# One kernel, two blocks of layers: pooling and a convolution's norm run inside the head norms, and a bias table is built inside the attention that reads it

## What is computed

```python
def _pool_branch(u, grid, pool_w, pool_scale):
    ...
    for g, win in enumerate(POOL_WINDOWS):
        ch = uf[..., g * POOL_GROUP:(g + 1) * POOL_GROUP]
        groups.append(_centred_mean(ch, axis, win) - ch)
    pooled = jnp.stack(groups, axis=-2)
    mixed = jnp.einsum('...gi,gio->...go', pooled, pool_w)
    return mixed.reshape(b, n, D_POOL) * pool_scale

def conformer_conv(a_val, a_gate, conv_w, conv_b, ln_g, ln_b):
    u = a_val * jax.nn.sigmoid(a_gate)
    u = dwconv(u, conv_w, conv_b)
    return jax.nn.silu(layer_norm(u, ln_g, ln_b))

    q = axial_rope(rms_norm(q, qn_g))
    k = axial_rope(rms_norm(k, kn_g))

def neighborhood_attn(q, k, v, kc, vc, rpb):
    ...
    bias = rpb[:, dr_idx[:, None, :, None], dc_idx[None, :, None, :]]
    s_win = jnp.einsum('brqhd,brkwhd->bhrqkw', qg, kb).astype(jnp.float32) * scale \
        + bias.astype(jnp.float32)[None]
```

## Time and profile before

| what | us |
|---|---|
| median of three executions | 6007.8 (6003.9 to 6013.1) |
| the profiled execution | 6002.6 |
| its span in the trace | 6000.8 |
| PE busy (share of the span) | 5150.4 (86%) |
| DVE busy | 3387.5 (56%) |
| ACT busy | 1902.3 (32%) |
| POOL busy | 1751.2 (29%) |

### The profile page before, as it was taken

One profiled execution on the slowest core, in us unless ns is written; L12 is line 12 of the kernel. 1 busy time (PEld: TensorE's weight loads), 2 busy tenths in 40 slices (PEclk: granted clock), 3 DMA queues, 4 the chain that ended last, 5 costly groups with the idle time before them and its releaser, 6 DMA issues. The chain is left out here.

```text
span 6000.8 us, 127551 instructions
## 1 busy us (share of the span) xinstructions
PE 5150.4 (86%) x55385; PEld 3990.6 (67%) x55385; DVE 3387.5 (56%) x5084; ACT 1902.3 (32%) x3017; POOL 1751.2 (29%) x1377
## 2 busy tenths in 40 slices
PE   6799999699998466587999857999988999979989
PEld 1488888488888355466888634555557788766667
DVE  2236656444444566467699246888864300057877
ACT  1224444133332443133211223444430300026652
POOL 1201111254443655024200004666642511100012
PEclk8899999799999788888999978999999999989999
DMA  6334434411211110365332231000045321131035
GB/s 204 104 110 151 148 140 149 139 60 52 64 54 59 64 57 26 119 198 153 104 107 94 78 129 45 22 17 17 13 152 167 102 77 68 70 105 63 31 113 161
DMA packets 430189, 568.20 MB, mean 95 GB/s; under 512 B 66870, under 2 KB 318646, under 8 KB 417166
## 3 DMA queue, kind: packets, MB, share of 16 engines
q1 hardware_dynamic: 365158, 387.20, 20.6%
q10 hardware_dynamic: 49272, 115.65, 5.0%
q0 software_dynamic: 15216, 57.44, 2.4%
HBM read 357.07 MB, written 203.12 MB: 93 GB/s over the span
## 5 line engine op out<-in xcount | busy, mean ns | idle before, releaser
L157 PE MATMUL p_bank<-p_hT_high,p_w_high 128*128 128x512 f32 (+1 forms) x2784 | 1053.0, 378 | 19.7 <-DVE p_w_low L151 15.8
L159 PE MATMUL p_bank<-p_hT_high,p_w_low 128*128 128x512 f32 (+1 forms) x2784 | 1044.8, 375 | 0.0
L158 PE MATMUL p_bank<-p_hT_low,p_w_high 128*128 128x512 f32 (+1 forms) x2784 | 1044.7, 375 | 0.0
L157 PEld LDWEIGHTS p_bank<-p_hT_high,p_w_high 128*128 128x128 f32 x2784 | 525.2, 189 | 123.1 <-DVE p_w_low L151 16.2
L159 PEld LDWEIGHTS p_bank<-p_hT_high,p_w_low 128*128 128x128 f32 x2784 | 525.1, 189 | 94.8
L158 PEld LDWEIGHTS p_bank<-p_hT_low,p_w_high 128*128 128x128 f32 x2784 | 525.5, 189 | 93.2
L2832 POOL TENSOR_TENSOR at_acc<-at_acc,at_p 128x512 f32<-128x512 f32 x256 | 423.9, 1656 | 144.1 <-ACT at_p L2770 122.6
L2770 ACT ACTIVATE at_p<-at_sc 128x1024 f32<-128x1024 f32 (+1 forms) x296 | 284.9, 1013 | 401.6 <-PE at_sc L2661 349.7
L1555 PE MATMUL rsc_db<-rsc_W,rsc_TK 64*64 64x64 f32 x8640 | 383.7, 219 | 6.2 <-issue 6.0
L2874 DVE TENSOR_REDUCE at_mx<-at_mb 128x2 f32<-128x1024 f32 (+1 forms) x280 | 342.3, 1222 | 81.3 <-PE at_mb L2672 79.2
L157 PE MATMUL o_bank<-o_w_high,o_m_high 128*128 128x512 f32 x800 | 314.4, 393 | 63.7 <-POOL o_m_low L151 63.7
(11 more groups left out here) (419 smaller groups left out, 10627.9 us busy)
## 6 DMA issues: line engine op xcount, KB each, us to landing
rsc_X<-rwkv_chunks SPq DMA_DIRECT2D x108, 320.0 KB, 4.7
pT<-p_o ACTq DMA_DIRECT2D x132, 256.0 KB
rwkv_chunks<-p_arr POOLq DMA_DIRECT2D x54, 512.0 KB, 5.4
o_z<-pT SPq DMA_DIRECT2D x50, 512.0 KB, 5.3
o_y<-y SPq DMA_DIRECT2D x50, 512.0 KB, 6.5
pT<-p_eo ACTq DMA_DIRECT2D x96, 256.0 KB
p_w<-in_w_in_dram SPq DMA_DIRECT2D x33, 512.0 KB, 4.3
x<-o_o ACTq DMA_DIRECT2D x32, 512.0 KB
```

Source lines behind the costliest of these rows:

```text
L157: nc.tensor.matmul(out, lhs[0], rhs[0], start=start, stop=False)
L158: nc.tensor.matmul(out, lhs[0], rhs[1], start=False, stop=False)
L159: return nc.tensor.matmul(out, lhs[1], rhs[0], start=False, stop=stop)
```

## The change

Three stages lose their own block.

- **pool** goes. Its work is a class `Pooling`, which `head_norm` calls ahead of its own work on each engine in the stage hn: first the pooling's loads, then item 0's, and so on. The second tile `u[1]` is loaded after the constants, with a semaphore of its own, and the results are written over the tiles `u`. PE uses the banks of the odd items; the wait for them (`released`) stands ahead of item 1.
- **cf** goes. Its work is a class `Conformer`, called the same way at the head of stage qk. Gates 2 to 4 move into the loop over the items, on ACT ahead of the squares of items 1 to 3 (`GATES_AT`). SP loads items 0 to 2, then issues the five stores of the chunks, each waiting for its gate, and only then loads anything else.
- The four pieces of the modulation move from pool to qk: SP issues their 8 loads behind the chunks' stores and ahead of the load of item 3; PE does piece 0 to 3 at the end of its turns 6 to 9, DVE adds the bias at the end of its turns 7 to 10, SP stores them last.
- **nat** goes. `one_hot` is loaded in four parts into tiles that the attention uses later, the raw biases come over ACT's queue, q, k and v are loaded right behind; PE and DVE build `bt` as before, in the banks of the scores; the scores of step 0 follow at once, and `bi` is made after the maxima of step 0 (steps 0 and 1 read `bt` only).

```diff
-def pool_branch(nc, PT, w, scale, inv_count, yT, later):
...
+class Pooling:
...
+    def loads(self, sp):
+        sp.wait_ge(self.zeroed, 3)
+        for t in range(2):
+            sp.dma_start(self.u[t][:, :, POOL_PAD:POOL_PAD + self.W],
+                         self.PT[t * P:(t + 1) * P, 0:SEQ].rearrange("p (r w) -> p r w", w=self.W)).then_inc(self.u_in[t], 16)
+            if t == 0:
+                sp.dma_start(self.cnt[:], self.inv_count).then_inc(self.const_in, 16)
+                sp.dma_start(self.sc[:], self.scale.rearrange("(t p) -> p t", p=P), allow_slow_non_contiguous=True).then_inc(self.const_in, 16)
                 for g in range(4):
                     h = g % 2 * HD
...
+                    sp.dma_start(self.wd[h:h + HD, g // 2, h:h + HD], self.w[g]).then_inc(self.const_in, 16)
+
+    def out(self, t):
+        return self.u[t][:].rearrange("p r w -> p (r w)")[:, 0:SEQ]
+
+    def stores(self, sp):
+        for t in range(2):
+            sp.wait_ge(self.scaled, 4 * (t + 1))
+            sp.dma_start(self.yT[t * P:(t + 1) * P, 0:SEQ], self.out(t)).then_inc(self.stored, 16)
...
+        for t in range(2):
+            dve.wait_ge(self.u_in[t], 16)
+            dve.wait_ge(self.const_in, 16 * 6)
...
-def head_norm(nc, name, items, mean_ones, gather, spread, rope=None):
+def head_norm(nc, name, items, mean_ones, gather, spread, rope=None, before=None, later=None):
...
+        first = before[0](nc, ctx, *before[1], banks[4:8])
+        MC = 384
+        PIECES = [c * MC for c in range(4, 3 * D // MC)] if later else []
...
+            mp = [*bank[1][1:4], bank[0][3]]
...
+                first.loads(sp)
                 load(0)
...
-                for n in range(2, NI):
+                load(2)
+                if later:
+                    sp.dma_start(cond[:, 0, :], mod_c[0].rearrange("(p k) -> p k", k=KT)).then_inc(cond_in, 16)
+                    sp.dma_start(cond[:, 1, :], mod_c_ctx.rearrange("(p k) -> p k", k=KT)).then_inc(cond_in, 16)
+                first.stores(sp)
+                for q, c in enumerate(PIECES):
+                    sp.dma_start(ms[q][:], mod_b[c:c + MC].partition_broadcast(2)).then_inc(mw_full[q], 16)
+                    sp.dma_start(mw[q][:], mod_w.rearrange("(p k) n -> p k n", k=KT)[:, :, c:c + MC]).then_inc(mw_full[q], 16)
+                for n in range(3, NI):
                     load(n)
+                for q, c in enumerate(PIECES):
+                    sp.wait_ge(mod_bias, q + 1)
+                    sp.dma_start(mod_out[:, c:c + MC], ms[q][:]).then_inc(mod_stored, 16)
+                first.finished(sp)
+                if later:
+                    sp.wait_ge(mod_stored, 16 * len(PIECES))
...
+                first.vector(dve)
                 dve.wait_ge(const_in, 16 * NCONST)
...
+                    q = n - (NI - 3)
+                    if 0 <= q < len(PIECES):
+                        dve.wait_ge(mod_sum, q + 1)
+                        dve.wait_ge(mw_full[q], 32)
+                        nc.vector.tensor_tensor(ms[q][:], mp[q][0:2, 0:MC], ms[q][:], ALU.add).then_inc(mod_bias, 1)
...
+                    if n == 1:
+                        first.released(pe)
...
+                first.tensor(pe)
                 pe.wait_ge(const_in, 16 * NCONST)
...
+                    q = n - (NI - 4)
+                    if 0 <= q < len(PIECES):
+                        pe.wait_ge(act_ready, 1)
+                        pe.wait_ge(mw_full[q], 32)
+                        for k in range(KT):
+                            mm = nc.tensor.matmul(mp[q][0:2, 0:MC], cond_act[:, k, :], mw[q][:, k, :], start=(k == 0), stop=(k == KT - 1))
+                        mm.then_inc(mod_sum, 1)
...
+                first.scalar(act)
+                if later:
+                    act.wait_ge(cond_in, 32)
+                    nc.scalar.activation(cond_act[:].rearrange("p k r -> p r k"), cond[:], ACT.Silu).then_inc(act_ready, 1)
...
+                    first.beside(act, n)
                     act.wait_ge(a_in[u], 16 * loads(n))
...
-def conformer(nc, ln_g, ln_b, mean_ones, yT):
+class Conformer:
...
+    GATES_AT = {1: 2, 2: 3, 3: 4}
...
+    def stores(self, sp):
+        for c, (t0, n) in enumerate(self.CHUNKS):
+            sp.wait_ge(self.acted, c + 1)
+            sp.dma_start(self.rows[:, :, t0:t0 + n], self.y[c][:, :, 0:n]).then_inc(self.stored, 16)
...
+    def beside(self, act, n):
+        if n in self.GATES_AT:
+            self.gate(act, self.GATES_AT[n])
...
+            if c == 2:
+                self.gate(act, 0)
+                self.gate(act, 1)
+
+    def gate(self, act, c):
+        n = self.CHUNKS[c][1]
+        act.wait_ge(self.normed, c + 1)
+        for t in range(self.NTL):
+            x = self.nc.scalar.activation(self.y[c][:, t, 0:n], self.y[c][:, t, 0:n], ACT.Silu, bias=self.pr[:, 1, t:t + 1], scale=self.pr[:, 0, t:t + 1])
+        x.then_inc(self.acted, 1)
...
-        with ExitStack() as ctx1:
-            s1 = Scope(nc, ctx1, "nat")
-            oh = s1.sb("oh", [64, ROW, P])
-            rp = s1.sb("rp", [64, NH, NDD])
-            raw = s1.sb("raw", [P, 64])
-            *ps, turned = s1.banks(5)
-            const_in, filled, rp_ready, prod, taken = (s1.sem(n) for n in ("const_in", "filled", "rp_ready", "prod", "taken"))
-            raw_in, raw_turned = s1.sem("raw_in"), s1.sem("raw_turned")
-            inner_ready, masked = s1.sem("inner_ready"), s1.sem("masked")
-            with nc.Block() as block:
-                @block.sync
-                def _(sp):
-                    sp.dma_start(idn[:], ident).then_inc(raw_in, 16)
-                    sp.wait_ge(filled, 1)
...
+        hot = [pt[u][0:64].rearrange("p a b c -> p (a b) c") for u in range(2)]
+        hot += [y[u][0:64].rearrange("p (n c) -> p n c", c=P) for u in range(2)]
+        table = [win[:, n // 2, n % 2, :] for n in range(4)]
...
+                sp.dma_start(idn[:], ident).then_inc(idn_in, 16)
+                for u in range(4):
+                    sp.dma_start(hot[u], one_hot[:, 16 * u:16 * u + 16, :]).then_inc(const_in, 16)
                 load_pair(0)
                 load_values(0)
...
+                pe.wait_ge(const_in, 16 * 4)
+                for n in range(ROW // 4):
+                    if n >= 4:
+                        pe.wait_ge(taken, n - 3)
+                    for i in range(4):
+                        x = nc.tensor.matmul(table[n % 4][:, i * P:(i + 1) * P], hot[n // 4][:, n % 4 * 4 + i, :], rp[:].rearrange("p h d -> p (h d)"),
+                                             start=True, stop=True)
+                    x.then_inc(prod, 1)
                 pe.wait_ge(zeroed, 1)
+                pe.wait_ge(taken, ROW // 4)
                 scores(0)
...
                 add(0)
                 maxima(0)
+                nc.vector.tensor_copy(bi[:], bt[:, :, 3:3 + R + 1, :]).then_inc(inner_ready, 1)
+                dve.wait_ge(inner_ready, 1)
+                nc.vector.memset(bi[0:64, :, R, :], MASK / SC).then_inc(masked, 1)
+                nc.vector.memset(bi[64:128, :, 0, :], MASK / SC).then_inc(masked, 1)
+                dve.wait_ge(masked, 2)
                 add(1)
...
+                act.wait_ge(filled, 1)
+                for half in range(2):
+                    act.dma_start(raw[0:NH * 15, 32 * half:32 * half + NDC], rpb.rearrange("h r c -> (h r) c")).then_inc(raw_in, 16)
                 keep_ctx(0)
...
-    pool_branch(nc, pT1, a["pool_w"][0], a["pool_scale"][0], a["inv_count"], y1, later[1])
...
-    head_norm(nc, "hn", items, a["head_mean"], a["head_gather"], a["head_spread"])
+    head_norm(nc, "hn", items, a["head_mean"], a["head_gather"], a["head_spread"], None,
+              (Pooling, (pT1, a["pool_w"][0], a["pool_scale"][0], a["inv_count"], y1)))
...
-    conformer(nc, a["ab_ln_g_2"][0], a["ab_ln_b_2"][0], a["mean_512"], y2)
...
-    head_norm(nc, "qk", items, a["head_mean"], a["head_gather"], a["head_spread"], (a["rope_cos"], a["rope_sin"], a["rope_swap"]))
+    head_norm(nc, "qk", items, a["head_mean"], a["head_gather"], a["head_spread"], (a["rope_cos"], a["rope_sin"], a["rope_swap"]),
+              (Conformer, (a["ab_ln_g_2"][0], a["ab_ln_b_2"][0], a["mean_512"], y2)), later[1])
```

More of the change, by code:

```diff
@@ L1283, with __init__ @@
 POOL_CH, POOL_PAD = 256, 8
-def pool_branch(nc, PT, w, scale, inv_count, yT, later):
+class Pooling:
     ROWS, W = SEQ // HD, HD
-    WP = W + 2 * POOL_PAD
-    with ExitStack() as ctx:
+    def __init__(self, nc, ctx, PT, w, scale, inv_count, yT, banks):
         s = Scope(nc, ctx, "pool")
[L1292 to L1310, removed]
-        with nc.Block() as block:
-            @block.sync
-            def _(sp):
[L1315 to L1320, removed]
@@ new lines, in tensor, with released @@
+    def tensor(self, pe):
+        for t in range(2):
+            pe.wait_ge(self.pooled_ready, t + 1)
+            for c in range(4):
+                if t:
+                    pe.wait_ge(self.scaled, c + 1)
```

(34 more changed lines are left out.)

334 lines of the change are left out of this document (126 added, 208 removed).

## The result

Four runs of the kernel after took 5942.7 to 5952.0 us, median **5946.2**; four of before, beside them, 5998.4 to 6013.1, median 6005.8. The forecast was 5957.7 (5936 to 5979) and faster.

What follows compares the result with a forecast made beforehand. TensorE was busy for 86% of the span, but barriers give each stage its own limit, with pool and cf chains of waits. Terms -66.9 + 29.4 - 28.2 + 21 + 7 - 12.4 = -50.1 gave 5957.7 us, range 5936 to 5979.

Steps and rivals of the forecast that it cites:

- Pool goes: Between p1 and rsc: rsc reads nothing that pool makes, so it starts where pool did, -66.9 us.
- Pooling at the head of hn: Start of hn: folding waits for DVE's window sums and starts 45.8 in, not 16.4, +29.4 us.
- Join of cf and qk: Head of qk: rotation constants are loaded early, so folding follows DVE's work on the chunks at once, -28.2 us.
- The gates: Gates 2 to 4 on ACT, between qk's roots and squares: hidden in ACT's idle time, nothing; uncovered, three would cost 16.
- Item 3 is late: In qk, item 3's load stands behind 6.3 MB of weights, so PE's sums of item 3 start later, +21 us.
- The pieces: End of qk, PE's turns 6 to 9: four modulation pieces of 5.24 each, partly hidden, +7 us.
- nat goes: Start of attention: first scores no longer wait for copies to `bi`, barrier and landing of q and k, -12.4 us.
- A: Rival in qk: item 3 is not late, sum -71.1, kernel 5937 us; chance 0.10.
- B: Rival in qk: pieces run at 1.2 GHz, 5.2 more each, about +20, kernel 5978 us; chance 0.13.
- C: Rival in qk: weights come at 154 GB/s, disturbed by POOL's stores, +24, kernel 5982 us; chance 0.07.
- D: Rival in qk: kernel slower, SP's queue holding item 3 back for 83 us; chance 0.03.
- E: Rival: untouched stages give the time back or joined stages start as late as before, 5996 to 6020 us; chance 0.04.

Runs made afterwards that it cites:

- e8: e7 with only the pads of `u` and the small matrix zeroed, counts loaded first, window sums not waiting for the matrix: ratio to before 0.9836, hn 149.85 us.
- e1: The kernel after with item 3's load issued ahead of the four weight loads in qk: ratio to before 0.9892, cf and qk 197.3 us.
- e2: The kernel after with the weight loads issued behind item 2's load, ahead of the chunks' stores: ratio to before 0.9867, cf and qk 187.2 us.
- e3: e2 with one matmul in place of eight in each modulation piece: executed once, cf and qk 181.3 us.
- e7: The kernel after with weights right behind the chunks' loads, item 3 ahead of the last chunk's store, pieces moved earlier: ratio to before 0.9831, cf and qk 176.9 us.

## Why the prediction was right

**Pool goes:** -66.9 to the tenth. The next stage, which reads nothing of it, starts as far behind p1 as pool did (7.6).

**Pooling at the head of hn:** +28.0 for +29.4. The mechanism is the one given (window sums, then folding, in one chain on DVE); the folding moved by 28.2. The sums started 14.8 after the first instruction, not 15.9, because the matrix landed 1 sooner. e8 shows that the chain sets the folding: 6.5 taken from its front bring the folding 6.4 forward. The rest of hn isn't the constant that it was taken for: it varies by some 3 either way, so the agreement of the whole stage to 1.4 is partly luck.

**Join of cf and qk:** the folding moved by 30.3 for 28.2. The other 2 lie in the chunks' own chain: DVE ends it 61.2 after the stage's start, where before it took 63.2. Why that chain got shorter wasn't looked into. The gates cost 0.6, not nothing. The argument (PE asks for square n only after item n - 2 is rotated) has no hold on square 1, since there is no item ahead of item 0, and gate 2 stands ahead of that square: PE waited 0.63 for it, which was one of the recorded signs of being wrong, if a small one. For gate 3 the argument held, with ACT still waiting 8.12 for PE before its root of item 2. The table load of 1.28 ahead of gate 4 is followed by its silu 1.30 after its start (3460.11, 3461.41), again with nothing behind it. The Trainium skill (ScalarE: Activation LUTs, What ACT_TABLE_LOAD costs) has 2.66 with a drain; the trace doesn't agree, here as in the earlier trace rows, and the measurement decides.

**Item 3 is late:** the sums of item 3 came 67.0 behind the folding in after and 46.5 before: +20.5, for +21. The mechanism and the size are right: PE's wait before them grew by 22.1, from 3.65 to 25.80, and square 3 began 26.7 behind the end of gate 4, where the sum had 26.0. (The "idle ACT of some 20" doesn't fit the prediction's own sum.) Against the 22.1, items 0 to 2 went 1.7 faster than before, which the sum didn't have: over item 0's sums PE's granted clock was 0.66 (5.54 us), before 0.57 (6.37). e1 and e2 show the cause and not only the coincidence: with the weights ahead of the need the wait falls by 20.7, with item 3 alone ahead most of it moves to item 4. The Trainium skill (DMA: Bandwidth & Descriptors, Two DMAs through the same engine are not ordered) says that within one queue of one DMA engine descriptors start in order; the trace agrees as far as it shows it, in that item 3, issued behind the weights, landed 14 after its issue at 373 GB/s, and in e1, issued ahead of them, 6 after it.

**The pieces:** +8.25 for +7, read from item 6's sums to the attention's first load (33.5 against 25.2); e3 shows the cause. Pieces 1 to 3 took 5.32, piece 0 took 7.48: until 3543.0 its granted clock was 0.50, as over item 6's sums ahead of it, and over piece 1 it was 1.00. The predicted end of piece 0 was 7.8 behind the start of those sums, and it was 8.6. (The 3.4 put down for eight records of 512 columns at full clock is 3.5 by the pieces' own 0.33 for 384, and 3.60 in after's trace; nothing hangs on it.)

**nat goes:** -13.4 for -12.4; the `one_hot` parts landed about 1 earlier than the whole did.

**What the sum missed.** Between the sums of item 3 and of item 6 after took 46.3 where before took 49.0 (-2.7). Most of it is one group of matmuls, the sums of item 4, in after and then before:

```profile
3508.48 3.72 PE L2311 MATMUL qk_bank<-qk_b,qk_ga 128*128 128x256 f32 x16 [3.65 <-DVE qk_a L2262]
...
3555.09 6.54 PE L2302 MATMUL qk_bank<-qk_b,qk_ga 128*128 128x256 f32 x16 [3.65 <-DVE qk_a L2261]
```

The granted clock was 1.00 over the first and 0.55 over the second, and it gave 2.8. Item 3's sums gave 0.9 (5.69 for 6.54), and item 4's rotation, at 6.32 for 5.34, took 1.0 back. That is the whole 2.7, and it can't be counted on: with the same instructions up to there, item 4's sums took 3.72 in e2 and 5.41 in e3. The terms that were worked out add up to -50.1 against -56.5 measured in their stages, and the untouched stages gave +1.9 in this pair of executions: 4.5 below the forecast. The other 7.0 of the 11.5 between forecast and median are the executions profiled: that of before took 5.2 less than its median of then, that of after (5948.0) 1.8 more than its own.

**The rivals.** A (item 3 not late) is ruled out by the 26.73; B by pieces of 5.32 (piece 0 alone ran in part at the lower clock); C by 373 GB/s; D by the wait's being 25.8 and not 83; E by every joined stage and by the +1.9 of the untouched ones. A to D were decided by single rows that the prediction had named.

## What to carry to other kernels

In these joins two stages in one block gave back idle time at their seam, and it could be read ahead from the first instruction of the later stage that the chain waits for. But all queues join too: list what each queue now holds between the seam and the next thing that is needed, in bytes at the measured rate, and put large loads that nobody waits for where the queue is ahead of its readers, not where it has just caught up. An edit of 1% is read by its stage, and where the rest of the stage varies (hn), by the instruction that the edit should move; the kernel's own time says only that it is there.

## What was not expected of the hardware

Stages with the same instructions vary from one execution to the next, and rsc with hg most: 1302.0 (e3), 1306.6 (e1), 1309.3 (e2), 1316.5 (after), 1321.6 (e7 and e8). So e7's profiled span, 5919.3, is longer than e2's, 5912.9, although its cf and qk are 10.3 shorter, and only the repeated runs show the order. The same stretch within hg (the twelfth of fourteen equal ones of rsc and hg), in the busy time by stretch of e3 and then of e7:

```profile
2101.90:2194.90 93.00, 65.55 (x2844) 56.79 (x2840) 71.02 (x118) 43.45 (x53) 49.27 (x28) 0.93 0.08 30
```

and

```profile
2122.90:2217.30 94.40, 66.49 (x2836) 57.64 (x2832) 68.50 (x121) 45.97 (x57) 49.27 (x28) 0.91 0.08 29
```

The stretch, with all but the same matmuls in it (2844 and 2836 records), takes 1.4 more, at a slightly lower granted clock (0.93, 0.91). Why the clock differs is open.

SP's issue of a transfer grew long when several MB were outstanding, though not evenly. In after the four weights' issues took 0.59, 0.55, 0.57 and 4.30, and those of the bias loads between them, of 3 KB each, 0.36, 0.58, 1.74 and 2.99. An instruction that follows on SP waits for that too: item 3 was issued 12.0 behind the first bias load, where eight issues at the shortest durations seen there (0.36 and 0.55) would have taken 4. That this delayed item 3's landing isn't shown, since the DMA engines were busy all that time (share 1.04).
